# Five raw slab places and four row places in the value stage, a later load of the hidden ring, and one low half moved in the stage before it

## What is computed

```python
def block(args):
    xb, ib, gb = args                                  # tokens, picked experts, gates
    hid = jnp.einsum('td,tkd->tk', xb, u[ib])
    act = jax.nn.gelu(hid, approximate=False) * gb
    return jnp.einsum('tk,tkd->td', act, v[ib])
...
x = layer_norm(DEEPNORM_ALPHA * x + ffn, ln_g[l, 1], ln_b[l, 1])
```

## Time and profile before

| | us |
|---|---|
| three runs | 3211.93, 3222.85, 3229.44 (median 3222.85) |
| profiled execution, its own time | 3225.26 |
| its span | 3223.5 |
| TensorE busy | 3129.9 (97%) |
| VectorE busy | 2665.3 (83%) |
| ScalarE busy | 1989.7 (62%) |
| DMA, mean over the span | 301 GB/s |

### The profile page before, as it was taken

The page is one execution under the profiler, slowest core; times in us unless marked ns, Lnnn a source line. Parts: engine busy times, 40 slices in busy tenths (PEclk is TensorE's granted clock), DMA queues, the critical chain, the costliest instruction groups (busy, mean ns, idle before and its releaser), DMA issues.

```text
span 3223.5 us, 51808 instructions
## 1 busy us (share of the span) xinstructions
PE 3129.9 (97%) x19468; PEld 2533.0 (79%) x19468; DVE 2665.3 (83%) x3291; ACT 1989.7 (62%) x3383; POOL 585.3 (18%) x266
## 2 busy tenths in 40 slices
PE   9999999999999999999999999999999999999998
PEld 8888878999999965566668887899999986555665
DVE  5785668998899888899987757898898988888997
ACT  4444555554899855566665545555599985556666
POOL 0000000013222223333310000011322123332330
PEclk9999999999999999999999999999999999999999
DMA  7554245789999989999984344588999999999996
GB/s 268 184 190 148 94 164 182 288 335 360 366 380 382 389 333 362 359 388 383 397 320 156 116 152 152 197 315 327 375 381 381 383 360 359 360 358 371 376 397 235
DMA packets 169220, 969.08 MB, mean 301 GB/s; under 512 B 18912, under 2 KB 52704, under 8 KB 55648
## 3 DMA queue, kind: packets, MB, share of 16 engines
q1 hardware_dynamic: 132192, 698.61, 58.5%
q0 software_dynamic: 36864, 268.45, 20.6%
HBM read 951.26 MB, written 15.73 MB: 300 GB/s over the span
## 4 chain that ended last, share of the span: by engine, by line
PE 39%; DMA 17%; DVE 9%; ACT 7%; issue 3%; ACTq 0%; DVEq 0%
PE ps L1069 38%; DMA raw<-in_v 8%; DVE halves L1967 4%; DMA raw<-in_u 3%; ACT wh L629 3%; DMA h_scratch<-hring 3%; DMA arena<-in_v,idx 2%; ACT hot_w L821 2%; DVE arena L2211 1%; DMA arena<-in_urows,idx 1%; DVE arena L1985 1%; DVE hot L2148 0%; ACT hring L806 0%; DMA hring<-h_scratch 0%; ACT cross L665 0%
## 5 line engine op out<-in xcount | busy, mean ns | idle before, releaser
L1069 PE MATMUL ps<-xx,wh 128*128 128x384 f32 (+1 forms) x5504 | 1326.5, 360 | 6.5 <-DVE xx L1802 4.7
L1967 DVE SCALAR_TENSOR_TENSOR halves<-raw,wh 128x2048 f16<-128x2048 f32 x508 | 1161.3, 2287 | 192.4 <-issue 133.5
L629 ACT ACTIVATE wh<-raw 128x2048 fp32r<-128x2048 f32 x508 | 970.8, 1911 | 262.5 <-DMA raw<-in_v 216.1
L1069 PEld LDWEIGHTS ps<-xx,wh 128*128 128x128 f32 x5504 | 964.5, 189 | 74.9 <-issue 6.7
L1069 PE MATMUL ps<-wh,act 128*128 128x512 f32 x3584 | 955.4, 405 | 17.0 <-ACT wh L629 16.7
L1069 PE MATMUL ps<-halves 128*128 128x192 f16 (+2 forms) x6144 | 798.1, 295 | 37.6 <-DVE halves L1967 37.4
L1069 PEld LDWEIGHTS ps<-wh,act 128*128 128x128 f32 x3584 | 673.5, 189 | 190.8 <-ACT wh L629 30.8
L1069 PEld LDWEIGHTS ps<-halves 128*128 128x128 f16 (+1 forms) x6144 | 448.4, 100 | 332.3 <-issue 223.1
L1758 POOL DMA_INDIRECT arena<-in_urows,idx x128 | 226.6, 1770 | 1804.2 <-DVE idx L2103 1015.5
L1758 POOL DMA_INDIRECT arena<-in_v,idx x128 | 349.9, 2733 | 716.3 <-DVE arena L2211 692.5
L1793 DVE TENSOR_TENSOR wl<-raw,wh 128x1024 fp32r<-128x1024 f32 x240 | 292.5, 1222 | 157.4 <-ACT wh L615 156.5
(11 more groups left out here) (239 smaller groups left out, 1847.8 us busy)
## 6 DMA issues: line engine op xcount, KB each, us to landing
raw<-in_u SPq DMA_DIRECT2D x256, 1024.0 KB, 7.5
raw<-in_v SPq DMA_DIRECT2D x256, 1024.0 KB, 7.4
raw<-in_w SPq DMA_DIRECT2D x118, 1024.0 KB, 4.9
h_scratch<-hring SPq DMA_DIRECT2D x128, 96.0 KB, 7.6
hring<-h_scratch SPq DMA_DIRECT2D x128, 96.0 KB, 7.6
arena<-in_memT SPq DMA_DIRECT2D x4, 512.0 KB, 7.2
raw<-in_w SPq DMA_DIRECT2D x4, 512.0 KB, 7.7
arena<-in_xT SPq DMA_DIRECT2D x4, 512.0 KB, 9.7
```

The costliest lines, as they stand in the source:

```text
L629: nc.scalar.activation(wh[:, j:j + 2, :], raw[:, n % RAW_SLABS, :].rearrange("p (e c) -> p e c", e=2), ACT.Copy, scale=W_UP if scaled_up(p ...
L1069: return nc.tensor.matmul(out, lhs, rhs, start=start, stop=stop, **kw)
L1967: v.scalar_tensor_tensor(out=wl16[:, j:j + 2, :], in0=raw[:, p // 2 % RAW_SLABS, :].rearrange("p (e c) -> p e c", e=2), scalar=W_UP, in1=w ...
```

## The change

Three things change.

1. In the value stage two more raw places (`raw_far`) and two more row places (`rows_far`) are laid into the space of `xx`. From slab 6 on the five raw places are used in turn, so slab k waits for the low half of slab k - 5 (slabs 6 and 7 wait until TensorE is done with slab 1). The rows 2, 3, 6, 7, ... of the value gathers go into the far places; rows 2 and 3 wait until TensorE is done with slab 1, and each later row n waits for row n - 4.
2. SyncE's loop issues the slab first, and the load of the hidden ring `LOAD_LAG` = 3 slabs later: `load(k)` stands after `slab(k + 3)`. The last three loads have no slab before them.
3. In `PAIR_FILL` one "S", the low half of up slab 2, moves from step 0 of the fourth pair to step 4 of the third.

```diff
+FAR, FAR_FROM = 2, 6
-STORE_LAG = 4
+STORE_LAG, LOAD_LAG = 4, 3
-PAIR_FILL = ([("L", "", "L", "", "L", "", "L", "")] * 2 + [("L", "L", "L", "L", "", "", "", "")]
-             + [("S", "S", "", "S", "S", "", "S", "S"), ("S",) * 8,
+PAIR_FILL = ([("L", "", "L", "", "L", "", "L", "")] * 2 + [("L", "L", "L", "L", "S", "", "", "")]
+             + [("", "S", "", "S", "S", "", "S", "S"), ("S",) * 8,
...
+def raw_places():
+
+    places, last, uses, turn = [], {}, collections.Counter(), 0
+    for n in range(P_END // 2):
+        k = value_slab(n)
+        if k is not None and k >= FAR_FROM and (k - FAR_FROM) % (FAR + RAW_SLABS) < FAR:
+            j = RAW_SLABS + (k - FAR_FROM) % (FAR + RAW_SLABS)
+        else:
+            j, turn = turn % RAW_SLABS, turn + 1
+        uses[j] += 1
+        places.append((j, uses[j], last.get(j)))
+        last[j] = n
+    return places
+def gather_places():
+
+    places, last, uses = [], {}, collections.Counter()
+    for n in range(4 * PAIRS):
+        j = n % (2 * PAIRS) - PAIRS
+        slot = (j - SLOTS) % (2 * SLOTS) if j >= SLOTS else n % SLOTS + SLOTS
+        uses[slot] += 1
+        places.append((slot, uses[slot], last.get(slot)))
+        last[slot] = n
+    return places
...
+    rows_far = nc.alloc_sbuf_tensor_at("rows_far", [P, SLOTS, D], F32, offset=xx_at + FAR * 2 * PC * 4)
+    rows_at = [rows_far[:, j, :] for j in range(SLOTS)] + gbuf
+    raw_far = nc.alloc_sbuf_tensor_at("raw_far", [P, FAR, 2 * PC], F32, offset=xx_at)
...
             n = p // 2
-            if n >= RAW_SLABS:
-                sp.wait_ge(lo_ready, split_by(n - RAW_SLABS))
-            sp.dma_start(raw[:, n % RAW_SLABS, :], src).then_inc(raw_full[n % RAW_SLABS], 16)
+            j, _, held = RAW_PLACES[n]
+            if j >= RAW_SLABS and value_slab(n) < FAR_FROM + FAR:
+                sp.wait_ge(piece_used, 2 * (n - value_slab(n)) + 4)
+            elif held is not None:
+                sp.wait_ge(lo_ready, split_by(held))
+            sp.dma_start(raw_slab(n), src).then_inc(raw_full[j], 16)
...
-            for k in range(RAW_SLABS + 1, S_EXP):
-                if k >= KEPT + BODY:
-                    load(k)
-                slab(v_in[row0 + k, :, :], v0 + 2 * k)
+            for k in range(RAW_SLABS + 1, S_EXP + LOAD_LAG):
+                if k < S_EXP:
+                    slab(v_in[row0 + k, :, :], v0 + 2 * k)
+                if k - LOAD_LAG >= KEPT + BODY:
+                    load(k - LOAD_LAG)
...
-            if n >= SLOTS:
-                pool.wait_ge(slot_free, n - (SLOTS - 1))
+            slot, _, held = GATHER_PLACES[n]
+            if slot < SLOTS and j < 2 * SLOTS:
+                pool.wait_ge(piece_used, (P_V0, P_V1)[n // (2 * PAIRS)] + 4)
+            elif held is not None:
+                pool.wait_ge(slot_free, held + 1)
```

More of the change, by code:

```diff
@@ L19 @@
+import collections
 import itertools
@@ L198, in split_by, with value_slab @@
     return 2 * n + 2 + (2 * n in PAIRED_FIRST + PAIRED_LAST)
+def value_slab(n):
+    for p0 in (P_V0, P_V1):
+        if p0 <= 2 * n < p0 + 2 * S_EXP:
+            return n - p0 // 2
+    return None
+def raw_places():
[10 more added lines that the diff above has]
+    return places
+RAW_PLACES = raw_places()
+def gather_places():
[7 more added lines that the diff above has]
+    return places
+GATHER_PLACES = gather_places()
 def rope_chunk(n):
@@ L410, in one_hot @@
         return rows.rearrange("p (j t) -> p t j", t=4)[:, t, :]
-    raw_full = [sem(f"raw_full{j}") for j in range(RAW_SLABS)]
+    raw_full = [sem(f"raw_full{j}") for j in range(RAW_SLABS + FAR)]
     half_in = [sem(f"half_in{n}") for n in range(2)]
@@ L459, in build @@
     sidx_ready, rep_ready, idx_ready = sem("sidx_ready"), sem("rep_ready"), sem("idx_ready")
-    gath_in = [sem(f"gath_in{j}") for j in range(SLOTS)]
+    gath_in = [sem(f"gath_in{j}") for j in range(2 * SLOTS)]
     slot_free, vacc_ready = sem("slot_free"), sem("vacc_ready")
@@ L486, in with_sink, with raw_slab, raw_landed @@
         return both_heads(s)[:, r, LATE_SINK:EARLY_AT] if late else both_heads(s)[:, r, EARLY_AT:EARLY_SINK + 1]
+    def raw_slab(n):
+        j = RAW_PLACES[n][0]
+        return raw[:, j, :] if j < RAW_SLABS else raw_far[:, j - RAW_SLABS, :]
     def raw_piece(p):
         n, e = half_of(p)
-        return raw[:, n % RAW_SLABS, e * PC:(e + 1) * PC]
+        return raw_slab(n)[:, e * PC:(e + 1) * PC]
+    def raw_landed(n):
+        j, use, _ = RAW_PLACES[n]
+        return raw_full[j], 16 * use
     block_cm = nc.Block()
@@ L611, in hi @@
             n, _ = half_of(p)
-            act.wait_ge(raw_full[n % RAW_SLABS], 16 * (n // RAW_SLABS + 1))
+            act.wait_ge(*raw_landed(n))
             if p in (2, 3):
@@ L627, in hi_slab @@
             n, j = p // 2, p % RING
-            act.wait_ge(raw_full[n % RAW_SLABS], 16 * (n // RAW_SLABS + 1))
-            nc.scalar.activation(wh[:, j:j + 2, :], raw[:, n % RAW_SLABS, :].rearrange("p (e c) -> p e c", e=2), ACT.Copy,
+            act.wait_ge(*raw_landed(n))
+            nc.scalar.activation(wh[:, j:j + 2, :], raw_slab(n).rearrange("p (e c) -> p e c", e=2), ACT.Copy,
                                  scale=W_UP if scaled_up(p) else 1.0).then_inc(hi_ready, 2)
@@ L1755, in gather @@
         def gather(rows_of, n, j):
-            if n >= SLOTS:
-                pool.wait_ge(slot_free, n - (SLOTS - 1))
-            pool.indirect_dma_start(out=gbuf[n % SLOTS], out_offset=None, in_=rows_of,
+            slot, _, held = GATHER_PLACES[n]
[3 more added lines that the diff above has]
+                pool.wait_ge(slot_free, held + 1)
+            pool.indirect_dma_start(out=rows_at[slot], out_offset=None, in_=rows_of,
                                     in_offset=bass.IndirectOffsetOnAxis(ap=idx[:, j:j + 1], axis=0))\
-                .then_inc(gath_in[n % SLOTS], 16)
+                .then_inc(gath_in[slot], 16)
         for layer in range(2):
@@ L1967, in low_slab @@
                 v.scalar_tensor_tensor(out=wl16[:, j:j + 2, :],
-                                       in0=raw[:, p // 2 % RAW_SLABS, :].rearrange("p (e c) -> p e c", e=2), scalar=W_UP,
+                                       in0=raw_slab(p // 2).rearrange("p (e c) -> p e c", e=2), scalar=W_UP,
                                        in1=wh[:, j:j + 2, :].bitcast(F32), op0=ALU.mult, op1=ALU.subtract)\
@@ L1975, in gathered @@
             def gathered(n):
-                dve.wait_ge(gath_in[n % SLOTS], 16 * (n // SLOTS + 1))
-                return gbuf[n % SLOTS]
+                slot, use, _ = GATHER_PLACES[n]
+                dve.wait_ge(gath_in[slot], 16 * use)
+                return rows_at[slot]
             def dot():
@@ L2098, in experts @@
                         if layer:
-                            dve.wait_ge(gath_in[(2 * PAIRS - 1) % SLOTS], 16 * ((2 * PAIRS - 1) // SLOTS + 1))
+                            slot, use, _ = GATHER_PLACES[2 * PAIRS - 1]
+                            dve.wait_ge(gath_in[slot], 16 * use)
                         own.mark(v.tensor_scalar(idx[0:NS, :], ps[0:NS, 7, 0:PAIRS], float(layer * KEYS * KEYS), None,
```

## The result

The changed kernel takes 3815.36 us (median of 4 runs, 3812.49 to 3817.89), the kernel before 3223.40 us beside it (3211.93 to 3229.44). The ratio is 1.187, with an interval of 1.184 to 1.190. The forecast was 3838 us, in a range of 3690 to 3990. The profiled execution has a span of 3815.9 us against 3223.5.

The account below looks back on a forecast made before the run. The prediction took TensorE, busy 97% of the span, to set the time in most stages. It summed 3225.3 - 30 (first halves) - 3 (up slab 2) + 640 (ring) + 8 (clock) = 3840, forecast 3838 us at the median, range 3690 to 3990.

Parts of the forecast that it names:

- The ring: Second halves of the value stages: late load, its reader, low half and next issue wait on each other in turn; +640 us.
- The landing: Ring load's time from issue to landing: 4.7 us without an accumulation, 7.2 us after one.
- the bound from below: Landing of 4.7 us, from eight loads each 0.37 us behind a slab at the value stage's end, gathers over.
- The first halves: First halves of the value stages: more places let transfers come in time, 4.30 us a slab; -30 us.
- the opening: Start of the value stage, injections and slow products behind them: stays as before, 4 us given back from the first halves' gain.
- Up slab 2: Up stage: TensorE's 3.11 us wait nearly goes, a wait for slab 3 comes; 1.67 us a layer left, -3 us in all.
- The clock: TensorE in the ring: about half the clock, costing only when the last slabs drain slow, some 4 us a stage; +8 us.
- That the ring never forms: Rival, second halves: something overlooked gives the load room, only the gains are left; 3190 us, 3%.
- Overtaking: Rival, ring: the 96 KB load doesn't wait for the 1 MB slab ahead and lands in 2.6 us; 3460 us, 4%.
- the half clock as a part of the ring: Rival, second halves: half clock adds 4.25 us in 112 intervals instead of lying beside the ring; +476, 4314 us, 3%.
- That the first halves gain nothing: Rival, first halves: no gain since the DMA is full; 3868 us, inside the range, no chance given.

Follow-up runs that it names:

- e5: The changed kernel with each load issued ahead of the slab that it stood behind, after the same wait; 3443.47 us, one run.
- e6: The changed kernel with all 64 accumulations and gathers of a value stage spread over slabs 2 to 63; 3684.69 us, one run.
- e9: The changed kernel with the load one slab behind and the low half of up slab 3 one step earlier; 3174.63 us, ratio 0.988 to before.
- e2: The changed kernel with the load two slabs behind, not three; 3371.91 us, ratio 1.046 to before.

## Why the prediction was right

**The ring.** Right in mechanism, place and count: 114 waits for 114 forecast. Its size was +640 us and 8 for the clock, measured +628. The sum gave 557.9 us for the part in the ring; 581.7 less 7 slabs at 4.25 us outside it is 552. Two small errors partly cancel: the sum gave all 26 accumulations a gather, where 4 let none go, and took 7.2 us for a landing beside one, where it is about 7.4.

**The landing.** Both values, chosen between bounds of 4.7 and 9.9 us, were close: 4.69 without a gather, 7.43 to 7.7 with one. What made the bound from below safe was that the trace had eight loads in the same place behind a slab. The four loads at 2.6 us, which look like the better reference for a load by itself, would have given 3460 us; they have no slab right ahead, and e5 shows what such an order gives, 1.91 us for the load and 3443 for the kernel.

**The first halves.** Right in sign, a little low in size: 36.1 us against 30. The step was the pace of 4.30 us, taken from the best DMA rates on the page, 383 to 397 GB/s, as if the DMA were full there. It was not: e6 moves 422 GB/s through a whole first half. What holds the changed kernel is TensorE, which is busy without a gap at 4.25 us a slab; with this pace and the same 4 us for the opening the sum gives 36, which is the prediction's own upper bound. What I did not see is that each kind of place alone is worth nothing.

**Up slab 2.** Forecast 1.67 us a layer; in the changed kernel 1.62 in the first and nothing in the second. The low half came as early as forecast. The step was that the slow products after the wait for slab 2, which the rows showed (2.38 against 1.49 us), were given no price behind the new wait for slab 3. What is left of it then was had in 6 of 18 passages.

**The clock.** It fell in the ring, to 0.71 to 0.86 and not to about a half, so this reading was wrong: TensorE works at either rate in one slab, 2.89 us for the eight short products (1.59 at full clock), 4.5 to 4.8 for the twelve long ones, which take 3.1 at full clock. It cost nothing that a row shows, since TensorE waited 216 us for low halves all the same. Of the 8 us for it at most some 2 can be there: the four halves give +591.9 us, up slab 2 takes off 1.6, and the spans differ by 592.4.

**The rivals.** That the ring never forms was refuted by the result itself. Overtaking fell with the landings of the changed kernel and with e5, the half clock as a part of the ring with the turns of 7.64 us and with e6. That the first halves gain nothing fell with their 36.1 us.

**The total.** The forecast of 3838 us was 23 above the measured 3815. The ring made it 12 too high, the clock and the first halves 6 each, and up slab 2 made it 1 too low.

## What to carry to other kernels

When a buffer gets more places, its wait moves back, and everything that stands behind this wait in the same queue gets another release time; count anew, for each transfer, after which instruction it is issued and which instruction reads it. Here one constant, three slabs where one kept the old room, turned a gain of 1.1% into a loss of 18.7%. In a ring like this one a small transfer that something waits for belongs ahead of a large one in its queue (e5: 372 us). Where two kinds of transfer are both short of places, try both together: here either alone gave nothing. And a saving of a wait is safe only if the wait that takes its place is short: in e9 (0.35 us) all of it stayed, in the changed kernel (2.43 us) that of one layer.

## What the runs showed of the hardware

- A load of 96 KB lands in 1.91 us when nothing is ahead of it (e5), in 4.7 us when it is issued 0.37 us behind a load of 1 MB in the same queue, and in 7.4 us when a gather of 1 MB runs beside both.
- The 16 DMA engines moved 422 GB/s of slabs and gathers together in a window of 100 us in e6, at a busy share of 1.01; in the changed kernel, where TensorE sets the pace, 393 at 0.99.
- Work that comes about every second slab fell in step with a ring that spans two turns, and so was paid in full and not by its average (e2).
- After the same wait of 2.4 us TensorE went on at full pace in one layer and slow in the other layer of one execution (1.49 and 2.39 us for 16 products), which decides on a gain of 1.6 us; over nine kernels it was full pace 6 times of 18.
